# Group norm at the end of an RWKV recurrence: variances spread over channels by one product, root and reciprocal taken on 128x512

## The chip, the cores and the metric

The kernel runs on one core of one Trainium2 chip (trn2). The metric is the device time of one launch in microseconds, the median of several runs.

## The reference, cut to what matters

One layer of a streaming encoder over 1024 tokens of 1024 channels: a hybrid time mixer (RWKV-7 beside stick-breaking attention), a norm, an MLP, a norm. The change touches one thing in the RWKV branch, the norm of each head's answer over its 64 channels, and what follows it:

```python
RWKV_HEADS = 8; HEAD_DIM = 64; GN_EPS = 64e-5

def _group_norm(y, g, b):
    mu = jnp.mean(y, axis=-1, keepdims=True)
    var = jnp.mean(jnp.square(y - mu), axis=-1, keepdims=True)
    return (y - mu) * lax.rsqrt(var + GN_EPS) * g.reshape(RWKV_HEADS, HEAD_DIM) + b.reshape(RWKV_HEADS, HEAD_DIM)

y = _rwkv7_scan(rh, heads(decay), kh, vh, -kk, kk * ah)
y = _group_norm(y, rw_gn_g, rw_gn_b)
y = y + jnp.sum(rh * kh * rw_rk, axis=-1, keepdims=True) * vh
y_a = (y.reshape(bsz, s_len, D_RWKV) * g) @ w_branch_a
```

## The kernel before, in words

The program is six phases one after another: the start (conditioning, first norm, first projections), the recurrence, stick-breaking attention, the merge of both branches, the output projection with its norm, and the MLP. Only the recurrence (`phase_recurrence`) is changed. It lies between about 140 and 528 us of the span.

Data lies with channels on the 128 partitions and tokens along the free dimension. A tile of 128 channels is two heads of 64. The recurrence has 512 channels, so four pairs of heads, and 1024 tokens, so two halves of 512: eight **turns**, 0 to 7, each for one pair of heads and 512 tokens. A turn is long and its work is pipelined over later turns by hand. In the code of turn t, `n` is t+1 (whose decays and keys are prepared), `l` is t-1 (whose chain of states is run, in eight steps `chain(l, c)` and `state(l, c)`), `ll` is t-2 (whose answers are centred, squared and summed to variances) and `lll` is t-3 (whose norm is closed). So turns 3 to 7 close the norms of turns 0 to 4. The last three are closed after turn 7, in a stretch where TensorE computes the values' projection (lines 1961, 192 products) in 24 thirds, with the steps left over between them (`steps`).

Each engine runs its own list in the order that its function `turn(t)` writes; there is no scheduler. A `wait(engine, t, name)` holds the engine, and everything behind it in its list, until the count of the semaphore `name` has come to turn t. Each turn also inverts the triangular blocks of its own tokens by four rounds in which TensorE and VectorE alternate: `correction(t, k)` and `corrected(t, k)` on TensorE (lines 1784 and 1793), `inverse(t, k)` on VectorE (lines 1490 and 1492, signals `Te` and `TTe`). `correction(t, k)` can't start before `inverse(t, k-1)` has signalled `Te`. Between them TensorE does pieces of a dense projection (line 1628) in turns 1 to 6; turn 7 has none.

The closing norm of a turn goes like this before the change:

- ScalarE copies the answers to `ysb`; TensorE `centre` (line 1691) takes each head's mean away; ScalarE writes `yc` (line 1214) and its squares into `ysb` again (line 1220).
- TensorE `variance` (line 1699), at the end of the turn: four products, each with 128 tokens of `ysb` as the stationary side and two columns of 0 and 1 as the moving side. They leave 128x8 sums in the bank `TL`: tokens on the partitions, a column for each head and block of 128 tokens.
- In the next turn, ScalarE `deviation` (line 1226) takes the square root on 128x8 into `ri`, behind `state_maps` and in front of `correction(t, 0)`, and VectorE `inverse_deviation` (line 1458) its reciprocal, in front of `state0`.
- TensorE `deviations`, by `spread` (line 1656): eight products with one column of `ri` broadcast to 64 as the stationary side and the identity as the moving side, which turn the 128x8 numbers into 128x512 in `TL`, a token's number in all 64 channels of its head. It stands behind `correction(t, 1)` and in front of `chain(l, 1)`.
- VectorE `normalised` (line 1465), between `state(l, 1)` and `inverse(t, 1)`, multiplies `yc` by `TL`. Later `gained`, `added` and `gated` (lines 1471, 1478, 1485) finish it, with the gate's product (`gate`, line 1715) from TensorE.

An fp32 product of 128x512 is two instructions in the trace, and so is each of the smaller fp32 products.

## Time and profile before

| | |
|---|---|
| median of 3 runs | 1754.0 us (1753.24 to 1755.06) |
| the profiled execution, its own time | 1754.57 us |
| its span, first to last instruction | 1752.8 us |
| busy: PE, PEld | 1654.6 us (94%), 863.8 us (49%) |
| busy: DVE, ACT, POOL | 764.3 us (44%), 561.3 us (32%), 452.3 us (26%) |
| mean granted clock of TensorE | 0.986 of full speed |

PE is TensorE's products, PEld its loads of the stationary side, DVE is VectorE, ACT ScalarE, POOL GpSimd, SP SyncE. "L1656" is line 1656 of the kernel. A row's `out<-in` names the tiles: `rw_tail` is the bank `TL`, `rw_state` the banks of the chain of states, `rw_invx` and `rw_inv` the banks of the inversion, `rec_ri` is `ri`, `rec_ysb` is `ysb`, `rec_yc` is `yc`, `rec_st` the states, `rec_X` and `rec_T` tiles of the inversion. The granted clock (PEclk) is 1.00 at 2.4 GHz and 0.50 at 1.2 GHz. The bracket at a row's end is how long its engine stood idle before it and what ended that.

### The profile page before, as it was taken

The page shows a single profiled execution, that of the slowest core. Times are in us where ns is not written, and L with a number is a line of the kernel's source. Part 1 is how long each engine was busy: PE and PEld are TensorE (multiplying, and loading weights), DVE is VectorE, ACT ScalarE, POOL GpSimd, SP SyncE. Part 2 cuts the span into 40 slices and gives each one's busy share as a digit, 9 for nine tenths or more (in the row PEclk, how much of TensorE's full clock was granted, in tenths as well). Part 3 has the DMA queues.
Part 4 walks back from the last instruction along what each step waited for, and adds up shares of the span by engine and source line. Part 5 has one row for each costly group of instructions (what it writes and reads, how often), then busy time and mean ns, then how long its engine had stood idle before and what let it go on. Part 6 is the DMA issues. An engine that isn't in the chain of part 4 may idle for free. (4 is left out here: it accounts for less than half of the span.)

```text
span 1752.8 us, 35509 instructions
## 1 busy us (share of the span) xinstructions
PE 1654.6 (94%) x15497; PEld 863.8 (49%) x15690; DVE 764.3 (44%) x1045; ACT 561.3 (32%) x883; POOL 452.3 (26%) x236
## 2 busy tenths in 40 slices
PE   4998889899999998899999999999999999999997
PEld 2455666666644555444444345444444444444443
DVE  5696555556425555312210388331323323222328
ACT  5323444444324555321212256321212112121200
POOL 2221322222110112022422123551423233232310
PEclk9999999999999999999999999999999999999999
DMA  9851001000101200411210211330202020212002
GB/s 358 285 175 32 15 6 38 4 27 27 28 25 49 61 1 1 137 44 36 72 36 24 96 49 37 103 129 21 85 20 76 24 72 26 70 36 84 1 0 97
DMA packets 105777, 109.75 MB, mean 63 GB/s; under 512 B 2592, under 2 KB 82610, under 8 KB 105394
## 3 DMA queue, kind: packets, MB, share of 16 engines
q1 hardware_dynamic: 105648, 107.82, 19.0%
q8 instruction: 107, 1.75, 0.4%
q14 instruction: 22, 0.18, 0.0%
HBM read 101.52 MB, written 4.19 MB: 60 GB/s over the span
## 5 line engine op out<-in xcount | busy, mean ns | idle before, releaser
L218 PE MATMUL tokens_ps<-a_hi,z 128*128 128x512 bf16 x878 | 228.5, 379 | 0.9
L674 PE MATMUL ff_ps<-ff_hi,c_lo 128*128 128x512 bf16 x503 | 190.6, 379 | 0.6
L674 PE MATMUL ff_ps<-ff_hi,c_hi 128*128 128x512 bf16 x501 | 189.9, 379 | 1.3 <-DVE z L2582 0.9
L674 PE MATMUL ff_ps<-ff_lo,c_hi 128*128 128x512 bf16 x501 | 189.9, 379 | 0.6
L2582 DVE TENSOR_TENSOR z<-ff_ps,z 128x512 f32<-128x512 f32 x128 | 88.3, 690 | 205.1 <-PE ff_ps L674 204.4
L2478 ACT ACTIVATE ff_r<-tokens_ps,cols 128x1024 f32<-128x1024 f32 x30 | 33.4, 1113 | 421.4 <-PE tokens_ps L218 414.4
L2404 POOL TENSOR_TENSOR z<-z 128x1024 bf16<-128x1024 f32 x28 | 62.1, 2219 | 345.5 <-ACT z L2400 345.5
L218 PEld LDWEIGHTS tokens_ps<-a_hi,z 128*128 128x128 bf16 x896 | 87.7, 98 | 105.7
L2570 DVE TENSOR_TENSOR ff_r<-ff_r 128x1024 f32<-128x1024 f32 x32 | 41.1, 1284 | 219.4 <-ACT ff_r L2478 219.4
L218 PE MATMUL tokens_ps<-a_lo,z 128*128 128x512 bf16 x438 | 131.1, 379 | 0.5
L195 POOL TENSOR_TENSOR mg_wlo<-mg_stage,mg_whi 128x1024 bf16<-128x1024 f32 x21 | 45.7, 2178 | 158.2 <-ACT mg_whi L191 158.2
L2515 POOL TENSOR_TENSOR c_lo<-ff_r,c_hi 128x1024 bf16<-128x1024 f32 x32 | 75.7, 2366 | 29.4 <-ACT c_hi L2482 29.4
L674 PEld LDWEIGHTS ff_ps<-ff_hi,c_hi 128*128 128x128 bf16 x512 | 50.1, 98 | 61.7 <-issue 1.3
L218 PE MATMUL mg_ps<-a_hi,mg_whi 128*128 128x512 bf16 x253 | 76.0, 381 | 4.4 <-POOLq L88 4.3
L674 PEld LDWEIGHTS ff_ps<-ff_hi,c_lo 128*128 128x128 bf16 x512 | 50.1, 98 | 60.4
L674 PEld LDWEIGHTS ff_ps<-ff_lo,c_hi 128*128 128x128 bf16 x512 | 50.1, 98 | 60.3
L218 PE MATMUL mg_ps<-a_hi,mg_wlo 128*128 128x512 bf16 x250 | 75.7, 383 | 0.3
L218 PE MATMUL mg_ps<-a_lo,mg_whi 128*128 128x512 bf16 x249 | 75.1, 381 | 0.4
L2128 DVE TENSOR_TENSOR mg_ga<-mg_ga,mg_ps 128x1024 f32<-128x1024 f32 x7 | 8.5, 1221 | 143.7 <-PE mg_ps L218 143.7
L805 DVE TENSOR_TENSOR_SCAN b_lo<-z,sb_ahead 128x256 f32<-128x256 f32 (+3 forms) x32 | 53.2, 1704 | 41.2 <-ACT z L909 41.2
L218 PEld LDWEIGHTS tokens_ps<-a_lo,z 128*128 128x128 bf16 x448 | 43.8, 98 | 52.9
L2520 POOL TENSOR_TENSOR ff_lo<-ff_st,ff_hi 128x1024 bf16<-128x1024 f32 x32 | 68.0, 2156 | 0.0
(395 smaller groups left out, 3114.2 us busy)
## 6 DMA issues: line engine op xcount, KB each, us to landing
ff_st<-w_ff SPq DMA_DIRECT2D x8, 2048.0 KB, 7.7
z<-w_ff SPq DMA_DIRECT2D x30, 512.0 KB, 4.0
ada_w<-w_ada SPq DMA_DIRECT2D x6, 2048.0 KB, 8.3
z<-w_in SPq DMA_DIRECT2D x18, 512.0 KB, 4.9
z<-w_ada SPq DMA_DIRECT2D x8, 1024.0 KB, 13.4
mg_stage<-w_in SPq DMA_DIRECT2D x16, 512.0 KB, 3.9
zs_stage<-w_in SPq DMA_DIRECT2D x8, 512.0 KB, 7.3
ada_w<-w_ada SPq DMA_DIRECT2D x4, 1024.0 KB, 13.5
```

Source lines behind the costliest of these rows:

```text
L195: pool.tensor_tensor(lo[u][:], stage[u][:], hi[u][:], ALU.subtract).then_inc(lo_ready[u], 1)
L218: last = pe.matmul(out[:, h * HALF:(h + 1) * HALF], w[:, kt, :], a[:, slot, h * HALF:(h + 1) * HALF], start=(x == 0 and y == 0), stop=(x = ...
L674: last = pe.matmul(out, a[:, slot, at], w[:, x, n], start=(x == 0 and y == 0), stop=(x == k - 1 and y == 2))
L805: dve.tensor_tensor_scan(prod[b][:, 0:nk][:, ::-1], m, masked, 1.0, ALU.mult, ALU.max).then_inc(s_scan, 1)
L2128: dve.tensor_tensor(ga[:], ga[:], ps[2][:], ALU.mult).then_inc(s_pa, 1)
L2404: pool.tensor_tensor(ff.lo[u], stage[u], ff.hi[u], ALU.subtract).then_inc(ff.lo_ready[u], 1)
L2478: act.activation(r[u][:], (wide if begun and t >= begun else ps1)[u][:], ACT.Relu, bias=g.cols[:, ds(gr * GT + (b1 + t), 1)]).then_inc(s_r ...
L2515: pool.tensor_tensor(g.c_lo[:, GT * par + t, :], r[u][:], g.c_hi[:, GT * par + t, :], ALU.subtract).then_inc(s_ulo[u], 1)
L2520: pool.tensor_tensor(lo2[par][:, k, :], st2[:, k, :], hi2[par][:, k, :], ALU.subtract).then_inc(s_o2, 1)
L2570: dve.tensor_tensor(r[u][:], r[u][:], r[u][:], ALU.mult).then_inc(s_sq[u], 1)
L2582: dve.tensor_tensor(acc, ps2[x % 4], acc, ALU.add).then_inc(s_acc, 1)
```

## The change

`variance` is one product of 128x512: the stationary side is `bones`, the 128x128 matrix that has 1 where row and column belong to the same head, and the moving side is `ysb`. Each channel of a head so gets the head's sum of squares, for every token. `deviation` takes the square root on 128x512, from `TL` back into `ysb`. `inverse_deviation`, `deviations` and `spread` go, with `ri` and the semaphore `rb`. `normalised` first takes the reciprocal of `ysb` on 128x512, in place, and then multiplies `yc` by `ysb`. `gate` waits for the root (`sd`) in place of `normalised`'s signal (`y1`), and `answers` waits for `y1` of two turns before in place of `var`, since `ysb` is in use until then. In the stretch after turn 7 the same calls go.

```diff
--- before.py
+++ after.py
@@ -972,7 +972,7 @@
         wc = [sb(f"wc{f}", (P, NC)) for f in range(2)]
         bt, kt_, bh, kh = (sb(n) for n in "bt kt bh kh".split())
         kn, vn = (sb(n, (P, NT, P)) for n in "kn vn".split())
-        rn, ri = [sb(f"rn{f}", (P, NB)) for f in range(2)], sb("ri", (P, NB))
+        rn = [sb(f"rn{f}", (P, NB)) for f in range(2)]
         W, mk = ([c[:, at:at + 2, :].rearrange("p a n -> p (a n)").bitcast(F32).rearrange("p (b x n) -> p b x n", x=2, n=CH)
                   for at in (PAIRS, PAIRS + 2)] for c in (g.c_hi, g.c_lo))
         NTd, NTm = sb("NTd", (P, NB, CH)), sb("NTm", (P, NB, 3, B))
@@ -986,7 +986,7 @@
                     "ch": NC, "S": NC}
         names = ("gs du draw dz dhi dlo vs vz vdif vcopy kkr sq lw sg la a cum cumE eN eE eI t k2 aN ss ssm rn AT RT BT KT wc rk BhT KhT M0 pp TT0 M1e NTd NTm TTe Te "
                  "M2 M2e X Xe TX X21 X21e TTm T12 T12e vnT vne knT kne bnT bne anT ane mv mve PQ PQa PQd ZG ze ge HY S0 ch S out ysb cen yc sqy "
-                 "var sd ri rb y1 y2 bo bv gm y3 y4 yhi ylo vw vhi vlo vmm vout").split()
+                 "var sd ri y1 y2 bo bv gm y3 y4 yhi ylo vw vhi vlo vmm vout").split()
         s = {n: nc.alloc_semaphore(f"rws_{n}") for n in names}
         DENSE = len(DENSE_STAGE)
         s_din = {d: nc.alloc_semaphore(f"rws_din{d}") for d in range(2, DENSE)}
@@ -1202,7 +1202,7 @@
                 if not inside(l):
                     return
                 wait(act, l, "out")
-                wait(act, l - 2, "var")
+                wait(act, l - 2, "y1")
                 for c2 in range(2):
                     act.activation(c8(ysb[l % 2])[:, c2::2, :], half4(HY[c2], 1), ACT.Copy).then_inc(s["ysb"], 1)
 
@@ -1223,7 +1223,7 @@
                 if not inside(l):
                     return
                 wait(act, l, "var")
-                act.activation(ri[:], TL[:, 0:NB], ACT.Sqrt, bias=g.misc(4), scale=1.0 / HD).then_inc(s["sd"], 1)
+                act.activation(ysb[l % 2][:], TL[:], ACT.Sqrt, bias=g.misc(4), scale=1.0 / HD).then_inc(s["sd"], 1)
 
             def high(ll):
                 if not inside(ll):
@@ -1451,18 +1451,14 @@
                 shifted(dve, 8, l)
                 dve.tensor_tensor(rk[l % 4][:], TL[:], zs(8, l), ALU.mult).then_inc(s["bv"], 1)
 
-            def inverse_deviation(l):
-                if not inside(l):
-                    return
-                wait(dve, l, "sd")
-                dve.reciprocal(ri[:], ri[:]).then_inc(s["ri"], 1)
-
             def normalised(ll):
                 if not inside(ll):
                     return
-                wait(dve, ll, "rb")
+                wait(dve, ll, "sd")
                 wait(dve, ll, "yc")
-                dve.tensor_tensor(yc[ll % 2][:], yc[ll % 2][:], TL[:], ALU.mult).then_inc(s["y1"], 1)
+                dve.reciprocal(ysb[ll % 2][:], ysb[ll % 2][:]).then_inc(s["ri"], 1)
+                wait(dve, ll, "ri")
+                dve.tensor_tensor(yc[ll % 2][:], yc[ll % 2][:], ysb[ll % 2][:], ALU.mult).then_inc(s["y1"], 1)
 
             def gained(ll):
                 if not inside(ll):
@@ -1515,7 +1511,6 @@
                 queries(l, 0)
                 for e in range(2):
                     dve.tensor_tensor(W[f][:, 4 * e:4 * e + 4, 0, :], half4(BAB[e], 1), over(incl, NT), ALU.mult).then_inc(s["M1e"], 1)
-                inverse_deviation(lll)
                 state0(l)
                 write_hats(t)
                 inverse(t, 0)
@@ -1570,7 +1565,6 @@
             queries(end, 1)
             queries(end, 0)
             state0(end)
-            inverse_deviation(end - 2)
             normalised(end - 2)
             state(end, 0)
             gained(end - 2)
@@ -1581,7 +1575,6 @@
             bonus(end - 1)
             for c in range(3, 7):
                 state(end, c)
-            inverse_deviation(end - 1)
             state(end, 7)
             normalised(end - 1)
             gained(end - 1)
@@ -1590,7 +1583,6 @@
             bonus(end)
             wait(dve, end, "bv")
             dve.memset(vd[0:1, :, 0:P], 0.0).then_inc(s["vz"], 1)
-            inverse_deviation(end)
             normalised(end)
             gained(end)
             added(end)
@@ -1650,13 +1642,6 @@
                     last = pe.matmul(TL[:, 2 * j:2 * j + 2], tmp[:, j * P:(j + 1) * P], g.const[:, CT["misc"], 0:2], start=True, stop=True)
                 last.then_inc(s["ss"], 1)
 
-            def spread(dst, small, done):
-                for j in range(NT):
-                    for e in range(2):
-                        last = pe.matmul(dst[heads[e], j * P:(j + 1) * P], small[:, 2 * j + e:2 * j + e + 1].to_broadcast([P, HD]), ident,
-                                         start=True, stop=True)
-                last.then_inc(s[done], 1)
-
             def chain(l, c):
                 if not inside(l):
                     return
@@ -1695,23 +1680,15 @@
                     return
                 wait(pe, l, "yc")
                 wait(pe, l, "sqy")
-                for j in range(NT):
-                    last = pe.matmul(TL[:, 2 * j:2 * j + 2], ysb[l % 2][:, j * P:(j + 1) * P], g.const[:, CT["misc"], 0:2], start=True, stop=True)
-                last.then_inc(s["var"], 1)
-
-            def deviations(ll):
+                pe.matmul(TL[:], bones, ysb[l % 2][:], start=True, stop=True).then_inc(s["var"], 1)
+
+            def gate(ll):
                 if not inside(ll):
                     return
-                wait(pe, ll, "ri")
+                pe.wait_ge(s["gs"], 16)
+                wait(pe, ll, "sd")
                 if inside(ll + 4):
                     wait(pe, ll + 4, "sg")
-                spread(TL, ri, "rb")
-
-            def gate(ll):
-                if not inside(ll):
-                    return
-                pe.wait_ge(s["gs"], 16)
-                wait(pe, ll, "y1")
                 pe.matmul(TL[:], g_s[:, ll // 2 * P:(ll // 2 + 1) * P], zgs[:, tok(ll)], start=True, stop=True).then_inc(s["gm"], 1)
 
             def bonus(l):
@@ -1850,7 +1827,6 @@
                     dense(2, 0, 8)
 
                 correction(t, 1)
-                deviations(lll)
                 chain(l, 1)
                 if t:
                     dense(2 * n, 20, 24)
@@ -1934,17 +1910,14 @@
             state_terms(end)
             answer_terms(end)
             steps = {1 + c: [lambda c=c: chain(end, c)] for c in range(NC)}
-            steps[0] = [lambda: deviations(end - 2)]
             steps[1] += [lambda: gate(end - 2)]
             steps[3] += [lambda: bonus(end - 1)]
             steps[4] += [lambda: centre(end - 1)]
             steps[6] += [lambda: variance(end - 1)]
-            steps[8] += [lambda: deviations(end - 1)]
             steps[9] = [lambda: outputs(end), lambda: gate(end - 1)]
             steps[11] = [lambda: bonus(end)]
             steps[12] = [lambda: centre(end)]
             steps[14] = [lambda: variance(end)]
-            steps[16] = [lambda: deviations(end)]
             steps[17] = [lambda: gate(end)]
             pe.wait_ge(s["vlo"], KT)
             for tt in range(TT):
```

On VectorE, turn 5. `rec_st` is the states of the chain, `rec_T` and `rec_TT` the inversion. Before:

```order
L1444 TENSOR_TENSOR rec_zt<-rw_inv,rec_ar 128x4x64
L1517 TENSOR_TENSOR c_hi<-rw_main,const 128x4x64 x2
L1458 RECIPROCAL rec_ri<-rec_ri 128x8
L1427 MEMSET rec_st 128x64
L1412 TENSOR_TENSOR rec_bh<-rec_bt,rec_wc 128x512
L1490 TENSOR_TENSOR rec_T<-rw_invx,rec_T 128x256
L1492 STREAM_TRANSPOSE rec_TT<-rec_T 128x256
L1496 TENSOR_TENSOR c_lo<-rw_main,const 128x512 x2
L1435 SCALAR_TENSOR_TENSOR rec_st<-rec_st,rec_wc,rw_state 128x64
L1417 TENSOR_TENSOR rec_kh<-rec_kt,rec_wc 128x512
L1435 SCALAR_TENSOR_TENSOR rec_st<-rec_st,rec_wc,rw_state 128x64
L1465 TENSOR_TENSOR rec_yc<-rec_yc,rw_tail 128x512
```

And from the last of these states on, after the change:

```order
L1435 SCALAR_TENSOR_TENSOR rec_st<-rec_st,rec_wc,rw_state 128x64
L1459 RECIPROCAL rec_ysb<-rec_ysb 128x512
L1461 TENSOR_TENSOR rec_yc<-rec_yc,rec_ysb 128x512
L1486 TENSOR_TENSOR rec_T<-rw_invx,rec_T 128x256
L1488 STREAM_TRANSPOSE rec_TT<-rec_T 128x256
```

The small reciprocal at the turn's start is gone, and one of 128x512 stands directly in front of the multiplication, with the inversion's next round behind both.

On TensorE, turn 5, from the products of the inversion's `correction(t, 1)` to the gate's. Before:

```order
L1784 MATMUL rw_invx<-rec_T,rec_NTm 32x32 x32
L1656 MATMUL rw_tail<-const,rec_ri 64x128 x8
L1670 MATMUL rw_state<-rec_st,rec_gt 64x64 x2
L1628 MATMUL rw_front<-a_hi,z 128x512 x2
L1628 MATMUL rw_front<-a_lo,z 128x512
L1628 MATMUL rw_front<-a_hi,z 128x512
L1793 MATMUL rw_invx<-rec_X,rec_TT 32x32 x32
L1772 MATMUL rw_main<-const,z 128x128 x4
L1670 MATMUL rw_state<-rec_st,rec_gt 64x64 x2
L1784 MATMUL rw_invx<-rec_T,rec_NTm 32x32 x32
L1715 MATMUL rw_tail<-z,rec_g_s 128x512
```

After:

```order
L1761 MATMUL rw_invx<-rec_T,rec_NTm 32x32 x32
L1655 MATMUL rw_state<-rec_st,rec_gt 64x64 x2
L1620 MATMUL rw_front<-a_hi,z 128x512 x2
L1620 MATMUL rw_front<-a_lo,z 128x512
L1620 MATMUL rw_front<-a_hi,z 128x512
L1770 MATMUL rw_invx<-rec_X,rec_TT 32x32 x32
L1749 MATMUL rw_main<-const,z 128x128 x4
L1655 MATMUL rw_state<-rec_st,rec_gt 64x64 x2
L1761 MATMUL rw_invx<-rec_T,rec_NTm 32x32 x32
L1692 MATMUL rw_tail<-z,rec_g_s 128x512
```

The eight spreading products are gone from between the correction and the chain's step, and nothing else moves.

## Rows read from the trace of the kernel before

**Rows 1.** Busy by stage: window, length, PE, PEld, DVE, ACT, POOL; PEclk, DMA, GB/s.
```profile
350.00:391.00 41.00, 38.22 (x1090) 27.25 (x1098) 23.05 (x49) 19.96 (x37) 9.74 (x7) 0.96 0.10 29
...
392.00:394.00 2.00, 2.00 (x96) 1.81 (x96) 0.00 (x0) 0.00 (x0) 0.00 (x0) 0.50 0.04 8
```

**Rows 2.** Whom TensorE waited for, 265 to 470 us: total, times, longest.
```profile
PE rw_front L1628 <- POOL z L1097: 4.5, 3, 1.5
```

**Rows 3.** Timeline of turn 5: start, duration, engine, line, operation, idle before.
```profile
363.78 1.09 PE L1656 MATMUL rw_tail<-const,rec_ri 128*64 128x128 f32 x16
...
364.81 0.33 PE L1670 MATMUL rw_state<-rec_st,rec_gt 64*64 64x64 f32 x4
...
365.19 0.28 DVE L1435 SCALAR_TENSOR_TENSOR rec_st<-rec_st,rec_wc,rw_state 128x64 f32<-128x64 f32 x1 [1.17 <-PE rw_state L1670]
...
365.38 0.68 DVE L1465 TENSOR_TENSOR rec_yc<-rec_yc,rw_tail 128x512 f32<-128x512 f32 x1
...
366.83 0.42 DVE L1490 TENSOR_TENSOR rec_T<-rw_invx,rec_T 128x256 f32<-128x256 f32 x1 [0.77 <-PE rw_invx L1793]
...
367.31 0.33 PE L1670 MATMUL rw_state<-rec_st,rec_gt 64*64 64x64 f32 x4
...
367.57 0.62 PE L1784 MATMUL rw_invx<-rec_T,rec_NTm 32*32 32x32 f32 x50
```

**Rows 4.** Groups by line and form on VectorE, whole run: busy us, mean ns.
```profile
L2287 DVE RECIPROCAL ou_rs<-ou_rs 128x1 f32<-128x1 f32 x16 | 2.6, 164 | 8.8 <-ACT ou_rs L2245 8.8
...
L1384 DVE RECIPROCAL rec_rn<-rec_rn 128x8 f32<-128x8 f32 x8 | 1.6, 203 | 0.3
...
L2552 DVE RECIPROCAL ff_rs<-ff_rs 128x1 f32<-128x1 f32 x8 | 1.2, 156 | 0.0
...
L568 DVE RECIPROCAL rs<-rs 128x1 f32<-128x1 f32 x8 | 0.9, 115 | 0.1
```

**Rows 5.** Timeline of turn 7, where TensorE waits for VectorE.
```profile
457.96 0.68 DVE L1452 TENSOR_TENSOR rec_rk<-rw_tail,z 128x512 f32<-128x512 f32 x1
...
458.80 1.10 PE L1691 MATMUL rw_tail<-rec_ysb,const 128*128 128x512 f32 x2 [0.19 <-DVE rec_rk L1452]
```

**Rows 6.** Timeline of turn 7, around the spreading.
```profile
445.44 1.98 PE L1656 MATMUL rw_tail<-const,rec_ri 128*64 128x128 f32 x16
...
447.34 0.48 PE L1670 MATMUL rw_state<-rec_st,rec_gt 64*64 64x64 f32 x4
...
447.87 0.28 DVE L1435 SCALAR_TENSOR_TENSOR rec_st<-rec_st,rec_wc,rw_state 128x64 f32<-128x64 f32 x1 [2.58 <-PE rw_state L1670]
...
449.76 0.60 ACT L1190 ACTIVATE rec_vn<-rw_main 128x512 f32<-128x512 f32 x1 [3.80 <-PE rw_main L1772]
...
449.92 0.75 PE L1784 MATMUL rw_invx<-rec_T,rec_NTm 32*32 32x32 f32 x64
```

**Rows 7.** Timeline of turn 7, the root on ScalarE and who waits behind it.
```profile
439.27 0.27 ACT L1226 ACTIVATE rec_ri<-rw_tail,const 128x8 f32<-128x8 f32 x1
...
439.87 0.32 PE L1793 MATMUL rw_invx<-rec_X,rec_TT 32*32 32x32 f32 x15 [0.75 <-ACT rec_X L1186]
```

**Rows 8.** Timeline of the stretch after turn 7.
```profile
469.00 1.09 PE L1656 MATMUL rw_tail<-const,rec_ri 128*64 128x128 f32 x16 [0.46 <-POOL z L1111]
...
472.24 0.28 DVE L1435 SCALAR_TENSOR_TENSOR rec_st<-rec_st,rec_wc,rw_state 128x64 f32<-128x64 f32 x1 [1.41 <-PE rw_state L1670]
...
474.90 0.33 PE L1670 MATMUL rw_state<-rec_st,rec_gt 64*64 64x64 f32 x4
```

**Rows 9.** Timeline of TensorE, the same products in turns 2 and 5.
```profile
189.57 0.69 PE L1808 MATMUL rw_main<-rec_ar,rec_bt 64*64 64x64 f32 x32
...
191.90 0.64 PE L1745 MATMUL rw_state<-rec_PQ,c_hi 64*64 64x64 f32 x32
...
350.52 1.13 PE L1808 MATMUL rw_main<-rec_ar,rec_bt 64*64 64x64 f32 x32
...
354.18 0.63 PE L1745 MATMUL rw_state<-rec_PQ,c_hi 64*64 64x64 f32 x32
```

More of the change, by code:

```diff
@@ L1697, in variance @@
                 wait(pe, l, "sqy")
-                for j in range(NT):
-                    last = pe.matmul(TL[:, 2 * j:2 * j + 2], ysb[l % 2][:, j * P:(j + 1) * P], g.const[:, CT["misc"], 0:2], start=True, stop=True)
-                last.then_inc(s["var"], 1)
-            def deviations(ll):
-                if not inside(ll):
-                    return
-                wait(pe, ll, "ri")
-                if inside(ll + 4):
-                    wait(pe, ll + 4, "sg")
-                spread(TL, ri, "rb")
+                pe.matmul(TL[:], bones, ysb[l % 2][:], start=True, stop=True).then_inc(s["var"], 1)
             def gate(ll):
@@ L1713, in gate @@
                 pe.wait_ge(s["gs"], 16)
-                wait(pe, ll, "y1")
+                wait(pe, ll, "sd")
+                if inside(ll + 4):
+                    wait(pe, ll + 4, "sg")
                 pe.matmul(TL[:], g_s[:, ll // 2 * P:(ll // 2 + 1) * P], zgs[:, tok(ll)], start=True, stop=True).then_inc(s["gm"], 1)
```

## The prediction

> **What bounds the kernel now.** I read the busy time by stage first. In turn 5, which stands for turns 3 to 6, TensorE is busy 38.2 of 41 us and VectorE 23.1 [rows 1]: TensorE sets the pace, VectorE has room on average. The waits of TensorE come second. Between 265 and 470 us the largest sum is 4.5 us in three waits for GpSimd at the start of a turn; for VectorE it waits once, 0.2 us [rows 5]. So before the change VectorE is never late. The third view is the timeline around the spreading, since a mean over a turn doesn't tell whether VectorE may be late at this one place. There the engines hand work to each other at short distances [rows 3]: the spreading starts at 363.78, the chain's step at 364.81, VectorE's state step at 365.19 (it had waited for it), its multiplication at 365.38, and TensorE needs the inversion's next round for its correction at 367.57. From the state step to that correction it is 2.38 us. What VectorE does in between must fit there.
>
> **What TensorE saves.** The spreading takes 364.81 - 363.78 = 1.03 us in a turn at full clock [rows 3], and 447.34 - 445.44 = 1.90 us in turn 7, where it ran at the lower clock [rows 6]. There are eight: turns 3 to 6, turn 7, and three after it. The variance product replaces four products with 128 columns of stationary side each by one of 128x512. An fp32 product of 128x512 is in these traces about as long as the spreading (1.10 us with its modelled end [rows 5]; the spreading 1.09 [rows 3]); the old variance is of the same kind, eight small instructions. I take no difference, 0.3 us either way in all. At the ends of turns 3 to 6 it is hidden anyway, for TensorE waits there for another engine, GpSimd in three of the four [rows 2].
>
> **The root on ScalarE.** It takes 0.27 us on 128x8 [rows 7]; a pass over 128x512 out of PSUM takes 0.60 [rows 6], so +0.33. In turns 3 to 6 TensorE's next product that waits for ScalarE comes later than that. In turn 7 it doesn't: TensorE waited for the copy right behind the root [rows 7]. There 0.33 us lie on the path. After turn 7 nothing of TensorE's is behind it.
>
> **The reciprocal on VectorE.** This is the unknown. The trace has no reciprocal of 128x512, but has small ones [rows 4]: 203 ns for 128x8, 164 and 156 for 128x1 in two places, 115 in a third. From one element to eight it grows by 39 to 47 ns, so 5.6 to 6.7 ns for each element. For 512 elements that makes 203 ns + 504 x 5.6 to 6.7 ns = 3.0 to 3.6 us; I take 3.3, the middle. The third place would give (203 - 115)/7 = 12.6 ns and 6.5 us, the upper bound. The lower is an operation that takes an element in the same time as the multiplication next to it: 0.68 us [rows 3]. I stay with the two rows that are nearest to each other, since slopes over seven elements are weak evidence and these two agree.
>
> The page "VectorE: DVE Perf Modes" of the Trainium skill, in "Walkthrough: the 8-slice pipeline in each mode", speaks against this change: the reciprocal is iterated, with a repeat count of 8, where an addition needs one stage. As an estimate from that page's 0.96 GHz it would be 8.3 ns an element, some 4.5 us, and the sum below would come to +9.4 in place of +3.4. The trace agrees that an element costs several times an ordinary one, but its slope is below 8.3 ns.
>
> **What it delays, in turns 3 to 6.** Behind the state step, VectorE now does: 0.19 us until the next operation starts (365.38 - 365.19 [rows 3]), 3.3 reciprocal, 0.68 multiplication (it reads SBUF in place of PSUM; GpSimd is idle then), 0.42 for the addition that signals `Te` (at 366.83 [rows 3]), and 0.16 from VectorE's end to TensorE's start (457.96 + 0.68 to 458.80 [rows 5]). That is 4.75 us in place of the 2.38: TensorE stands 2.37 us longer there. But it had reached the chain's step 1.03 us sooner. Net +1.34 a turn, 4 x 1.34 = **+5.4**. What is queued behind on VectorE (state steps, the cumulative sum, later rounds) moves by the same amount within 0.2 us, and so do ScalarE and GpSimd, which feed on it. So I see nothing that gives it back at the turn's end: GpSimd's late weights there follow ScalarE, and ScalarE follows TensorE.
>
> **Turn 7.** From the state step at 447.87 to the correction at 449.92 it is 2.05 us [rows 6]: 4.75 - 2.05 - 1.90 = +0.80, with the root's 0.33 **+1.1**.
>
> **After turn 7.** TensorE has dense products, and the spreads go: 3 x 1.03 = **-3.1**. What hides the reciprocal: the first one stands in front of the state step that released the chain's next step at 474.90. The multiplication would start about 471.5 (root's end about 468.1, plus 3.3), and the state step be done by 472.4, while TensorE comes to that next step at 474.90 - 1.03 = 473.87 [rows 8]: 1.4 us to spare. The second and third reciprocal stand behind the last state steps, and their results are needed 4 us or more later. So the cover holds up to a reciprocal of about 4.7 us; beyond, each further microsecond costs one.
>
> **Sum.** +5.4 + 1.1 - 3.1 = +3.4 us, and 5 us for each microsecond of the reciprocal: +1.9 at 3.0 us, +4.9 at 3.6. It breaks even at 2.6 us. Then the clock. In turn 6 TensorE ran at half clock for some microseconds (0.50, that is 1.2 GHz [rows 1]), after a wait of 1.5 us [rows 2] and before small products. The same products take 191.90 - 189.57 = 2.33 us at full clock and 354.18 - 350.52 = 3.66 in turn 5 after such a wait [rows 9]: 1.3 us for a fall. The new wait in turns 3 to 6 is from 367.31 + 0.33 - 1.03 = 366.61 to 367.57 + 1.34 = 368.91 [rows 3], 2.3 us, longer than those. I expect one or two falls in five turns, +2.0, between none and four (+5.2). Total +5.4. The sum stands against the profiled execution, 1754.57 us: 1760.0. The median of the runs is 0.57 lower, 1754.0, so the forecast is **1759.4 us**.
>
> **Rivals.** *One: the reciprocal is an ordinary pass.* If the slope of rows 4 is only start-up and 128x512 takes 0.68 us, the list behind the state step is 2.13 us, shorter than 2.38, and all savings count: 4 x -1.03, in turn 7 -1.90 + 0.33, after it -3.1, together -8.8: **1745.2 us**, faster. It decides below 2.6 us of reciprocal. For it: 115 to 203 ns are mostly fixed time, and VectorE's wide operations all lie at 0.7. Against: two slopes that agree at about six times the usual. Chance 0.13. The same page, in "The TRN2 errata", has a fixed cost and one element a cycle for VectorE's SBUF operations, which by its formula is 0.59 us for 512.
>
> *Two: it is slower still*, 4.5 us or up to 6.5. Then 3.4 + 5 x 1.2 = +9.4, with the falls +11.4, **1765.4 us**; at 6.5 us +16.0 more than at 3.3, 1.9 after turn 7, with falls 1777. For it: the third row of rows 4; against: its other two. Chance 0.12.
>
> *Three: the new wait is partly a gift.* TensorE's waits at the starts of turns (4.5 us [rows 2]) and its short stops for nothing visible could shrink by what it stands elsewhere, where their causes run ahead; that would take 2 to 5 us off: **1755.5 us**, level, perhaps below before. Against: those causes hang on TensorE themselves, as far as I followed them. Chance 0.13.
>
> The forecast's own case has 0.62, and runs from 1755.9 (3.0 us, no fall) to 1764.1 (3.6 us, four falls).
>
> **How the numbers follow.** A measurement of this kernel tells 0.2%, 3.5 us, from no change. Of the forecast's case 0.40 lies above that and 0.22 within. Rival one is faster (0.13), rival two slower (0.12), rival three 0.04 faster, 0.06 within, 0.03 slower. Together 0.17, 0.28, 0.55. The range 1751 to 1767 takes in the whole first case, most of rival three and rival two up to some 4.7 us, and leaves out rival one and the top of two, 0.19.
>
> **What would show it.** In the profile after: eight reciprocals of 128x512 at 3.0 to 3.6 us; no rows of 128*64 products into `rw_tail`; in turns 3 to 6 a wait of TensorE's correction for VectorE's addition of 2.0 to 2.7 us; distance from turn to turn 1.3 us longer, more where PEclk shows a fall; the stretch after turn 7 shorter by 3 us; every later phase unchanged. Wrong it would be with a reciprocal below 2.6 us, or with that wait there and the turns no longer.

## The result and the profile after

The changed kernel takes 1772.8 us (median of 4 runs, 1769.61 to 1776.29), the kernel before 1754.3 us on the same chip: a ratio of 1.0106, 95% interval 1.0086 to 1.0126. That is slower, as forecast, but by 18.4 us where 5.4 were forecast, and above the range. The profiled execution took 1772.95 us. Its page, the head and the instruction queue of the DMA section:

```profile
span 1771.2 us, 35345 instructions
...
PE 1675.3 (95%) x15514; PEld 853.9 (48%) x15514; DVE 784.3 (44%) x1045; ACT 565.8 (32%) x883; POOL 452.6 (26%) x236
...
q8 instruction: 123, 2.02, 0.5%
```

VectorE works 20 us more. TensorE's busy time reads 20.7 us higher, though its work became less. That can't be read as a rise, for the two traces don't hold the same share of the products. A product and its weight load come in pairs, and here both count 15514, while before the change 193 of the products have no record:

```profile
PE 1654.6 (94%) x15497; PEld 863.8 (49%) x15690; DVE 764.3 (44%) x1045; ACT 561.3 (32%) x883; POOL 452.3 (26%) x236
```

The one profile of the kernel before (with idle instructions, below) that has all its records shows 1678.0 us.

The last line of the page above counts packets and MB of the queue that brings the instructions; the same line of the kernel before is this:

```profile
q8 instruction: 107, 1.75, 0.4%
```

The program became shorter by 357 TensorE instructions, and fetched 16 packets more. The prediction does not use this line.

The groups of VectorE and ScalarE between 265 and 535 us (line, operation, form, times | busy us, mean ns):

```profile
L1459 DVE RECIPROCAL rec_ysb<-rec_ysb 128x512 f32<-128x512 f32 x8 | 26.8, 3347 | 8.8 <-ACT rec_ysb L1226 8.8
...
L1461 DVE TENSOR_TENSOR rec_yc<-rec_yc,rec_ysb 128x512 f32<-128x512 f32 x8 | 5.5, 691 | 0.3
L1226 ACT ACT_TABLE_LOAD x5 | 6.4, 1283 | 0.1
L1226 ACT ACTIVATE rec_ysb<-rw_tail,const 128x512 f32<-128x512 f32 x8 | 5.5, 686 | 0.8 <-PE rw_tail L1683 0.7
```

The reciprocal takes 3.35 us (forecast 3.3), the root 0.69 (0.60). Whom TensorE waited for between 265 and 490 us (total, times, longest), which answers to [rows 2]:

```profile
PE rw_invx L1761 <- DVE rec_T L1486: 11.4, 5, 3.3
PE rw_front L1620 <- POOL z L1097: 3.6, 3, 1.2
```

The first line is the new wait of the forecast, in all five turns. The timeline of turn 5 shows it, and what follows ([rows 3] are its counterparts):

```profile
368.74 3.35 DVE L1459 RECIPROCAL rec_ysb<-rec_ysb 128x512 f32<-128x512 f32 x1
372.12 0.69 DVE L1461 TENSOR_TENSOR rec_yc<-rec_yc,rec_ysb 128x512 f32<-128x512 f32 x1
372.73 0.42 DVE L1486 TENSOR_TENSOR rec_T<-rw_invx,rec_T 128x256 f32<-128x256 f32 x1
...
373.20 0.99 PE L1761 MATMUL rw_invx<-rec_T,rec_NTm 32*32 32x32 f32 x64 [2.01 <-DVE rec_T L1486]
374.13 2.08 PE L1692 MATMUL rw_tail<-z,rec_g_s 128*128 128x512 f32 x2
```

TensorE stands for 2.01 us, and the gate's product behind it takes 2.08 us. By the windows before and from there on (length, PE busy, PEclk, DMA, GB/s) the clock had fallen to 1.2 GHz for most of 4 us:

```profile
365.00:373.00 8.00, 6.18 (x209) 1.00 0.02 4
373.00:377.00 4.00, 3.80 (x72) 0.57 0.00 0
```

Where the 18.4 us lie is read from landmarks, operations that both kernels have: the 128x8 reciprocal of each turn, the closing memset, the first LayerNorm reciprocal after the output projection, and the first one after the MLP. Before the change (times, ns, first and last start):

```profile
L1384 DVE RECIPROCAL rec_rn<-rec_rn x8: 203/203/203, 154.8 to 419.2; 128x8 f32<-128x8 f32 x8
L793 DVE MEMSET sb_ahead<- x1: 805/805/805, 528.3 to 528.3; 128x896 f32 x1
L2287 DVE RECIPROCAL ou_rs<-ou_rs x16: 162/164/165, 998.4 to 1085.7; 128x1 f32<-128x1 f32 x16
L2552 DVE RECIPROCAL ff_rs<-ff_rs x8: 155/156/158, 1710.1 to 1748.0; 128x1 f32<-128x1 f32 x8
```

After it:

```profile
L1384 DVE RECIPROCAL rec_rn<-rec_rn x8: 203/203/204, 154.7 to 430.6; 128x8 f32<-128x8 f32 x8
L793 DVE MEMSET sb_ahead<- x1: 805/805/805, 539.1 to 539.1; 128x896 f32 x1
L2260 DVE RECIPROCAL ou_rs<-ou_rs x16: 163/164/166, 1007.7 to 1095.0; 128x1 f32<-128x1 f32 x16
L2525 DVE RECIPROCAL ff_rs<-ff_rs x8: 154/156/158, 1728.4 to 1766.4; 128x1 f32<-128x1 f32 x8
```

At the end of the recurrence the change is 10.8 us behind, 9.3 after the output projection, and 18.3 after the MLP. (The part between the first two took 468.6 to 471.3 us in the 18 profiles, so the 1.5 us there are spread.) So there are **two losses of about the same size**: one in the recurrence, and one of 9.1 us in the MLP, of whose code the diff touches nothing. There TensorE has two waits that the kernel before has not, 170 us apart, each directly behind the first two products of the loop's body:

```profile
1298.82 1.01 PE L218 MATMUL tokens_ps<-a_lo,z 128*128 128x512 bf16 x2 [2.38 <-issue]
1469.25 1.01 PE L218 MATMUL tokens_ps<-a_lo,z 128*128 128x512 bf16 x2 [2.64 <-issue]
```

and low clock behind each:

```profile
1299.00:1304.00 5.00, 5.00 (x18) 0.72 0.01 3
...
1469.00:1474.00 5.00, 4.75 (x15) 0.66 0.01 3
```

### The profile page after: what moved, and what is told of

It reads as the page before. It is cut to its first block and busy times, and to the rows that moved or that the text cites. A ratio compares the mean times of both kernels' runs of the same rounds, so it can differ in the third digit from the quotient of the medians.

```text
span 1771.2 us, 35345 instructions
## 1 busy us (share of the span) xinstructions
PE 1675.3 (95%) x15514; PEld 853.9 (48%) x15514; DVE 784.3 (44%) x1045; ACT 565.8 (32%) x883; POOL 452.6 (26%) x236
## 3 DMA queue, kind: packets, MB, share of 16 engines
q8 instruction: 123, 2.02, 0.5%
## 5 line engine op out<-in xcount | busy, mean ns | idle before, releaser
L218 PE MATMUL tokens_ps<-a_hi,z 128*128 128x512 bf16 x896 | 232.8, 381 | 0.4 <-issue 0.4
L674 PE MATMUL ff_ps<-ff_hi,c_hi 128*128 128x512 bf16 x512 | 194.0, 379 | 0.9 <-DVE z L2555 0.9
L674 PE MATMUL ff_ps<-ff_lo,c_hi 128*128 128x512 bf16 x512 | 194.0, 379 | 0.0
L218 PE MATMUL tokens_ps<-a_lo,z 128*128 128x512 bf16 x448 | 134.7, 383 | 5.0 <-issue 5.0
L1620 PE MATMUL rw_front<-a_hi,z 128*128 128x512 bf16 x224 | 76.5, 396 | 3.9 <-POOL z L1097 3.6
```

What stands on the lines that cost most here:

```text
L218: last = pe.matmul(out[:, h * HALF:(h + 1) * HALF], w[:, kt, :], a[:, slot, h * HALF:(h + 1) * HALF], start=(x == 0 and y == 0), stop=(x = ...
L674: last = pe.matmul(out, a[:, slot, at], w[:, x, n], start=(x == 0 and y == 0), stop=(x == k - 1 and y == 2))
L1620: mm = pe.matmul(unit_bank(u)[:], w_part[:, kt, :], a_part[:, kt, h * HALF:(h + 1) * HALF], start=(x == 0), stop=(x == 3 * KT - 1))
```

## The theories

**Theory A, the place of the code.** The change takes 88 fp32 products and, by a count of the program, five wait instructions out of TensorE's stream. The rows count two passes a product (x16 for eight in [rows 3]), each with its weight load, so four instructions: 88 x 4 + 5 = 357. Everything behind moves forward by these. The MLP's loop is 1581 instructions by the same count and runs three times, so it jumps back twice: the two waits. 2.02 MB in 123 packets are 16.4 KB each, which is 256 instructions if one has 64 bytes, and 1581 is 6 x 256 + 45: the loop touches 7 such pieces, or, if it starts in one of the last 44 places of a piece, 8. Two jumps that fetch 8 pieces each would be the 16 packets more. **Theory B**: the loop loses it by something else that the change does.

The Trainium skill, "Runtime: NRT & Kernel Launch", section "Instruction fetch mechanics", gives TensorE 128 KiB for instructions, refilled in blocks of 256, and says that a taken branch forces a fetch when its target isn't in the current window of two pages; it counts the crossing of a block as mostly hidden. The block size agrees with the packets. By the window of two pages every jump of this loop would stall, which the runs below don't bear out. By the 128 KiB, which would be 8 blocks, a loop that touches 8 would fit; that is not borne out either, if the start that stalls is one that touches 8. How much a jump costs the page doesn't say, the runs below do.

For the recurrence, **theory one** is the forecast's: VectorE is late at one place of the turn because of the 3.35 us. **Theory two**: the loss comes from the root, from the missing products, or from the code's place.

The kernel before was timed again on the chip of each of these runs, at medians of 1754.8 to 1755.2 us; the ratios are to these.

## First four: code restored, reciprocal out, reciprocal early

Idle TensorE instructions ("fillers") in `phase_start`, where TensorE waits anyway, put the later code back. A 32x32 product is four instructions. Of two `wait_ge` one is left as an instruction of its own, of six three, and a single one adds none:

```diff
+            for fill in range(89):
+                quarter = slice(32 * (fill % 4), 32 * (fill % 4) + 32)
+                pe.matmul(ada_ps[1][quarter, 0:32], g.const[quarter, CT["ident"], quarter], g.const[quarter, CT["ident"], quarter], start=True, stop=True)
+            for fill in range(2):
+                pe.wait_ge(s_const, 16)
```

> The change, with 357 TensorE instructions that compute nothing needed put into phase_start, where TensorE is idle for about 14 us: every later TensorE instruction stands again where it stood before the change, which had removed 357. Two theories share the 18.4 us that the change cost. Of both, the recurrence keeps its +10.8 (end of the phase 539 against 528 us). Theory A, the MLP loop lost its 9 us by where its instructions lie: from the first MLP reciprocal (1007.7 after, 998.4 before) the lead stays the same to the end, the waits of the loop's first product on issue (5.4 us each at most) are gone, and the time is 1763.5 (1762 to 1765). Theory B, the loop lost it by something else that the change does (a clock that stays lower, DMA queues): the waits stay, 1772.8 as the change itself.

Measured: 1764.8 us (1761.1 to 1766.0), ratio 1.0051 [1.0034, 1.0067]. The MLP's stretch, from first to first landmark, is 711.7 us, as before the change (720.8 in the change), and the queue has 107 packets. The loss is gone with every instruction of the change still there, so **B falls**; the next run makes it without the change.

> The kernel before, with 155 idle TensorE instructions in phase_start: modulo 256 instructions (16 KB, what one packet of the instruction queue carries) every later instruction then lies as it does in the change, which has 357 fewer. Theory A with a rule of 16 KB pieces: the MLP loop shows the issue waits and the time is 1763 (+9). Theory A without such a rule (the absolute place, or the order of fetches, decides): anything from +0 to +9. Theory B, placement does nothing: 1754.3, within 1 us of before.

38 products and six waits in the kernel before: 1763.5 us, ratio 1.0049 [1.0033, 1.0066]; nothing that computes had changed. Its recurrence ends 2.3 us earlier than in the kernel before, its MLP stretch is 719.7 us. It waits at both jumps, 2.44 and 1.97 us; the first, and the queue:

```profile
1287.82 1.01 PE L218 MATMUL tokens_ps<-a_lo,z 128*128 128x512 bf16 x2 [2.44 <-issue]
```

```profile
q8 instruction: 125, 2.05, 0.5%
```

The MLP's loss is so made without the change, and taken from it: **theory A holds.** The next kernel leaves the reciprocal out and multiplies by the deviation itself, so it computes something else:

```diff
-                dve.reciprocal(ysb[ll % 2][:], ysb[ll % 2][:]).then_inc(s["ri"], 1)
-                wait(dve, ll, "ri")
```

> As the filled change, but the 128x512 reciprocal is left out: the closing norm multiplies by the deviation instead of its inverse, every TensorE instruction is the same. Theory one, the reciprocal is what TensorE waits for in turns 3 to 7: each of these turns gets 3.3 us of VectorE back, no wait of the correction product on inverse(t, 0) beyond 1 us, no half clock behind it; recurrence ends some 6 us before that of before (turns -1.03 each and the end -3.1), 1747 (1744 to 1750). Theory two, the loss comes from elsewhere (the missing spreading products leave gaps, the wide root on ScalarE): less than half of the recurrence's +10.8 comes back, 1758 or more.

Measured: 1752.4 us, ratio 0.9987 [0.9978, 0.9997]. The time is above the 1744 to 1750, but the stretch it speaks of is right: from the landmark of turn 0 to the end of the phase 367.4 us, against 373.6 in the kernel before (-6.1) and 381.6 with the reciprocal. Eight reciprocals cost 14.2 us there. TensorE's wait for VectorE is gone, and of the five stretches of low clock between 265 and 500 us one is left, of 11 us where it had 15. **Theory one holds**: the root and the missing products are in this kernel too. What the expectation missed lies outside the recurrence: its landmark of turn 0 comes 2.0 us later than in the kernel before, and the part from the memset to the output projection took 1.1 us more. Both lie within the spread of single executions: that landmark comes at 153.9 to 158.9 us in the 18 profiles, and at 156.8 and 154.9 in two of one kernel.

In the last of the four, the root comes before `state_maps` on ScalarE and the reciprocal at the very start of VectorE's turn:

```diff
-                state_maps(l)
                 deviation(lll)
+                state_maps(l)
...
+            def inverse_deviation(l):
+                if not inside(l):
+                    return
+                wait(dve, l, "sd")
+                dve.reciprocal(ysb[l % 2][:], ysb[l % 2][:]).then_inc(s["ri"], 1)
...
             def turn(t):
...
+                inverse_deviation(lll)
                 wait(dve, t, "M0")
```

> As the filled change, but the root of a finished turn stands first on ScalarE and its 128x512 reciprocal first on VectorE, where VectorE waits about 6 us for M0 at the start of the next turn; the same work is done. Theory one (it is the place of the 3.345 us, not their amount, that costs): TensorE's wait on inverse(t, 0) falls to at most 0.5 us, the recurrence ends about 2 to 6 us before that of before, 1748 (1745 to 1753). Theory two (VectorE has no slack in a turn, the 3.3 us must be paid anywhere): as the filled change, 1762 to 1764.

Measured: 1754.1 us, ratio 0.9994 [0.9983, 1.0005]. That is 1 us above the expected range. Of the 12.3 us between the filled change and the one without a reciprocal the place alone gives back 10.6, with all eight reciprocals done. The order shows a price of its own (TensorE's waits, 265 to 490 us):

```profile
PE rw_invx L1775 <- ACT rec_gt L1205: 4.0, 2, 2.6
```

ScalarE's copy, which TensorE waits for here, had itself waited for VectorE. The longer of the two, in turn 7:

```profile
435.17 3.35 DVE L1464 RECIPROCAL rec_ysb<-rec_ysb 128x512 f32<-128x512 f32 x1 [4.21 <-ACT rec_ysb L1232]
438.44 0.69 DVE L1512 TENSOR_TENSOR rec_NTd<-rw_main,rec_rn 128x256 f32<-128x256 f32 x2
...
440.75 0.41 DVE L1450 TENSOR_TENSOR rec_zt<-rw_invx,rec_ar 128x256 f32<-128x256 f32 x1
...
441.20 0.38 ACT L1205 ACTIVATE rec_gt<-rw_invx 128x256 f32<-128x256 f32 x1 [4.85 <-DVE rec_zt L1450]
```

In turns 3 and 7 the early reciprocal reaches into the start of the inversion on VectorE, and TensorE pays 1.4 and 2.6 us for it.

## Four more: pieces or place, width, one-instruction root

> The change with 101 filler instructions instead of 357: TensorE's instructions after the filler lie at another absolute place than before the change (256 fewer), but at the same place within their 256-instruction, 16 KB pieces. Theory A with pieces (the MLP loop of 1581 instructions touches 7 pieces or 8, and only 7 stay loaded across a jump back): no issue wait at the two jumps back, some 106 packets on the instruction queue, 711.7 us from the first MLP reciprocal to the first closing LayerNorm reciprocal as before the change, time 1763 (1761 to 1765), perhaps 1 us less than with 357 fillers, which cost 2.2 us where they stand. Theory A by absolute place: the waits come back, 720 us for that stretch, 1771 or more.

25 products and two waits. Measured: 1761.2 us (1759.1 to 1766.8), ratio 1.0032 [1.0018, 1.0047]; MLP stretch 711.7 us, 106 packets. It is the place within the piece, and not the absolute place. Fewer fillers did not bring the landmark of turn 0 forward (158.3 us, 157.0 with 357), so the 2.2 us that I had put down to them are not theirs.

> Root and reciprocal early in the turn, with 101 fillers instead of 357. With pieces: the MLP stretch stays 711.7 us and the smaller filler gives back 1 to 1.6 us: 1752.8 (1751 to 1754.5), just below the kernel before. By absolute place: 1761.

Measured: 1752.7 us, ratio 0.9981 [0.9968, 0.9994], MLP stretch 711.7 us. As the piece rule had it.

```diff
-                dve.reciprocal(ysb[ll % 2][:], ysb[ll % 2][:]).then_inc(s["ri"], 1)
+                dve.reciprocal(ysb[ll % 2][:, 0:HALF // 2], ysb[ll % 2][:, 0:HALF // 2]).then_inc(s["ri"], 1)
```

`HALF` is 512.

> The filled change with only half of each reciprocal done (columns 0 to 255; the other half is multiplied by the deviation itself), everything else the same. Between 1764.8 with the whole and 1752.4 with none. Theory one, TensorE waits for VectorE at the same point of every turn as soon as VectorE has more work: the time follows the width, 1.67 of 3.34 us, so half of the 12.4 us comes back, 1758.6 (1757.5 to 1760). Rival, VectorE has a slack of 1 to 1.7 us in a turn and the clock falls only behind a long wait: nearly all comes back, 1754 or less.

Measured: 1753.4 us, ratio 0.9996 [0.9986, 1.0006]. The expected 1758.6 was wrong, and the rival holds: half the reciprocal costs nearly nothing. Turns 3 to 6 together take 163.2 us, the same as with none. VectorE has a slack there, and only what goes beyond it is paid. The waits that are left (265 to 490 us):

```profile
PE rw_invx L1767 <- DVE rec_T L1492: 2.4, 4, 0.6
```

The last of the four changes one function name and drops the reciprocal:

```diff
-                act.activation(ysb[l % 2][:], TL[:], ACT.Sqrt, bias=g.misc(4), scale=1.0 / HD).then_inc(s["sd"], 1)
+                act.activation(ysb[l % 2][:], TL[:], ACT.Abs_reciprocal_sqrt, bias=g.misc(4), scale=1.0 / HD).then_inc(s["sd"], 1)
...
-                dve.reciprocal(ysb[ll % 2][:], ysb[ll % 2][:]).then_inc(s["ri"], 1)
-                wait(dve, ll, "ri")
```

> The change with 101 fillers, where ScalarE takes the inverse root in one instruction (reciprocal square root of the same 128x512) instead of the root, and VectorE's reciprocal goes. TensorE's and ScalarE's instructions keep their number and place. Theory one: as without the reciprocal, recurrence 6 us shorter than before the change, 1751 (1749.5 to 1753) with the smaller filler. Rival: the new function takes longer than 0.69 us or needs a table load (1.28 us each) more often than the root, which had 5: 1753 to 1760. Its accuracy is open.

Measured: 1750.1 us, ratio 0.9971 [0.9962, 0.9981]. The function costs what the root did, with as many table loads (here in the version with 52 fillers):

```profile
L1232 ACT ACTIVATE rec_ysb<-rw_tail,const x8: 681/687/687, 271.3 to 500.1; 128x512 f32<-128x512 f32 x8
L1232 ACT ACT_TABLE_LOAD  x5: 1283/1283/1283, 270.0 to 430.2; - x5
```

## The edge of the piece, and three quarters of the width

> The one-instruction inverse root without any filler. Piece rule (8 pieces touched by the MLP loop instead of 7): every gain of the recurrence stays, but 16 packets more, two issue waits of about 2.5 us at the jumps back and 720.5 us instead of 711.7 in the MLP stretch: 1758.5 (1757 to 1760), slower than before the change although the recurrence is 6 us shorter. If the filler had helped for another reason: 1750 or less, since its own cost goes.

Measured: 1758.6 us, ratio 1.0016 [1.0006, 1.0025]; MLP stretch 718.4 us, 123 packets, waits at both jumps:

```profile
PE tokens_ps L218 <- issue: 4.5, 2, 2.3
```

> The same with 52 fillers. The runs so far (loop at instruction 112 of a piece: free; at 11: stalls, body of 1581 = 6 pieces and 45) leave 45 starts in 256 that touch an 8th piece; 44 fillers or more are then enough whatever the unknown offset. Piece rule: no stall, 711.7 us in the MLP stretch, 1749.7 (1748 to 1751.5). If it needs the old place: 1758 to 1759.

Measured: **1743.4 us** (1742.6 to 1744.3), ratio 0.9931 [0.9915, 0.9948]; MLP stretch 711.7 us, 105 packets. No stall, as expected; the recurrence is faster still than expected, of which more below.

> The kernel before with 200 idle TensorE instructions; 155 of them had brought the MLP stall (+8 us). 45 more carry the loop's start past the edge of the piece. Piece rule: the stall is gone again, MLP stretch 711.7 us, time 1756 (1754.5 to 1757.5, the filler's own 1 us). Rival, any shift away from a lucky place stalls, or a later place stalls more: 1763.

Measured: 1755.1 us, ratio 1.0001 [0.9992, 1.0011]; MLP stretch 711.7 us, 107 packets. 155 fillers stall, 200 don't. By the rule of pieces that must be so, for the 45 instructions between them are one more than the 44 places that touch an eighth piece. Where exactly these places begin and end no run shows: one start was tried that stalls and five that don't (45, 52, 76, 101 and 153 instructions further on, taken within a piece). Of the 18 profiles those three whose loop starts in the same place of a piece (the change, one_step_root_0, before_shifted) have an MLP stretch of 718.4 to 720.8 us, all the others 711.7.

> Filled change, 384 of the reciprocal's 512 columns (2.51 of 3.34 us), the rest multiplied by the deviation itself. With the half TensorE waited 0.6 us a turn for inverse(t, 0), with the whole 2.2; here 1.4 us. Theory with clock falls (a wait above some length is followed by 4 us at half clock, worth 1.6 us; five such in the whole, one in the half): four or five falls, 1761 (1759.5 to 1762.5). Theory without: only the waits grow, 4 to 5 turns by 0.84 us: 1757.3 (1756 to 1758.5).

Columns 0 to 383. Measured: 1757.9 us (1751.5 to 1760.4), ratio 1.0012 [1.0000, 1.0025]. TensorE waits 1.41 us in each of turns 3 to 6, as expected, but the clock falls behind one of these waits only, and the time lies in the range without falls. Two of the waits, and with the whole reciprocal the first of them:

```profile
286.82 0.85 PE L1767 MATMUL rw_invx<-rec_T,rec_NTm 32*32 32x32 f32 x64 [1.41 <-DVE rec_T L1492]
370.09 0.95 PE L1767 MATMUL rw_invx<-rec_T,rec_NTm 32*32 32x32 f32 x64 [1.41 <-DVE rec_T L1492]
```

```profile
285.82 1.08 PE L1767 MATMUL rw_invx<-rec_T,rec_NTm 32*32 32x32 f32 x64 [2.20 <-DVE rec_T L1492]
```

The windows around these waits, turns 3 to 6, with three quarters:

```profile
284.00:290.00 6.00, 4.59 (x147) 1.00 0.02 5
328.00:334.00 6.00, 5.30 (x150) 1.00 0.01 3
371.00:375.00 4.00, 4.00 (x16) 0.57 0.02 4
414.00:420.00 6.00, 6.00 (x154) 1.00 0.01 3
```

and with the whole:

```profile
285.00:289.00 4.00, 3.18 (x70) 0.57 0.01 4
330.00:334.00 4.00, 3.83 (x69) 0.60 0.00 0
374.00:378.00 4.00, 3.67 (x16) 0.57 0.01 4
419.00:422.00 3.00, 2.67 (x9) 0.51 0.00 0
```

Behind 2.2 us of waiting the clock fell in all four turns, behind 1.4 in one of four. Turns 3 to 6 take 174.3 us with the whole and 167.2 with three quarters. Of the 7.1 us between them 3.2 are waits (4 x 0.8, from 1.41 to 2.21); the other 3.9 go with three more falls, **1.3 us each**, the figure that the forecast had taken from [rows 9].

## What was left of the recurrence

> The change itself with 52 fillers. MLP stretch 711.7 us by the piece rule. If the start of the recurrence's code is worth 6 to 7 us: 1755 (1753.5 to 1757); if that gain belongs to the one-instruction root alone or to that chip: 1761 as with 101 fillers.

Measured: 1761.9 us, ratio 1.0037 [1.0025, 1.0049], as with 101 fillers. MLP stretch 711.7 us.

> The kernel before with the same 52 fillers. If the start of the recurrence is what counts and not its length: 1748 to 1750; if the place of every piece edge inside the turns counts (they lie otherwise here, 357 instructions more in the turns): anything between 1750 and 1757, most likely 1754.8.

Measured: 1752.9 us, ratio 0.9987 [0.9971, 1.0003]. Within the noise of no effect.

> The one-instruction root with 76 fillers, halfway between 52 (1743.4) and 101 (1750.1). If placement moves the recurrence's time steadily: 1746.5 (1745 to 1748.5); if it goes by steps: 1743.5 or 1750.

Measured: 1747.6 us, ratio 0.9952 [0.9938, 0.9966].

> The same kernel as one_step_root_52, on the chip of the three others of this call: 1743.4 (1742.5 to 1745) if the gain is the code's, 1749 to 1750 if it was the chip's.

Measured: 1745.6 us, ratio 0.9945 [0.9929, 0.9962]. Neither bound of the expectation: 2 us above the first time, still 4.5 below 101 fillers. The ratios go from 0.9931 and 0.9945 over 0.9952 to 0.9971 with 52, 76 and 101 fillers, so the start of the code seems to matter to this kernel by some 4.5 to 7 us (76 fillers lie in the range of a steady move); the change and the kernel before show no such gain with 52. TensorE's waits for nothing visible, in front of the correction (235 to 535 us), first with 52 and then with 101 fillers:

```profile
PE rw_invx L1765 <- issue: 2.0, 2, 1.3
```

```profile
PE rw_invx L1765 <- issue: 5.6, 6, 1.4
```

fit with that, but which instruction stalls on which fetch the runs did not show.

The stretches in one table (us; filler instructions ahead of the recurrence; the phase from the landmark of turn 0 to its end). They are those of one profiled execution each, which can lie some us from the median of its kernel (with the change and 101 fillers it took 1766.8 us, with the one-step root and none 1754.6):

| kernel | fillers | turns 3 to 6 | phase | MLP stretch | median |
|---|---|---|---|---|---|
| before | 0 | 166.4 | 373.6 | 711.7 | 1754.3 |
| the change | 0 | 178.6 | 384.5 | 720.8 | 1772.8 |
| the change | 52 | 173.8 | 379.5 | 711.7 | 1761.9 |
| the change | 101 | 176.4 | 382.4 | 711.7 | 1761.2 |
| the change | 357 | 174.3 | 381.6 | 711.7 | 1764.8 |
| 3/4 reciprocal | 357 | 167.2 | 375.3 | 711.7 | 1757.9 |
| 1/2 reciprocal | 357 | 163.2 | 369.2 | 711.7 | 1753.4 |
| no reciprocal | 357 | 163.2 | 367.4 | 711.7 | 1752.4 |
| early | 357 | 165.6 | 371.3 | 711.7 | 1754.1 |
| one-step root | 0 | 162.2 | 367.9 | 718.4 | 1758.6 |
| one-step root | 52 | 159.8 | 361.5 | 711.7 | 1743.4 |
| one-step root, again | 52 | 160.7 | 364.5 | 711.7 | 1745.6 |
| one-step root | 76 | 159.3 | 366.5 | 711.7 | 1747.6 |
| one-step root | 101 | 163.4 | 368.3 | 711.7 | 1750.1 |

In the change, fillers shorten the phase by 2 to 5 us too. So of the recurrence's 10.8 us some 8 are the reciprocal's net effect (6 to 9 in the three filled versions), and the rest, 2 to 5, goes with the place of the code or with the spread of single profiles; these two I can't tell apart.

## Why the prediction was wrong, step by step

- **The reciprocal**: 3.3 us taken, 3.35 measured, from two slopes over seven elements. Over the 504 further elements the slope is 6.2 ns. By the repeat count of the Trainium skill, "VectorE: DVE Perf Modes", section "Walkthrough: the 8-slice pipeline in each mode", it would have been 8.3. Rivals one and two had rested on other durations, and are out. Right.
- **The new wait**: 2.0 to 2.7 us forecast; 1.69, 2.21, 2.01 and 2.21 in turns 3 to 6 (and 3.25 in turn 7). Right in three of four turns.
- **Turns 3 to 6**: +5.4 and, with the falls, up to +7.4 was the sum. With the later code in its old place they are 7.9 longer (7.3 and 10.0 in the other two filled versions); in the change itself 12.2. The mechanism is right, and for the filled change the sizes too: four falls of the clock in these turns against two before the change, at 1.3 us each, turn the +5.4 into +8.0. In the change itself the clock falls five times there, which makes +9.3; 2.9 us stay open. The break-even at 2.6 us, which was that of the whole sum, came a little too high: with 2.51 us of reciprocal the sum gives about half a microsecond below the kernel before, and the ratio is 1.0012 [1.0000, 1.0025], so 0 to 4 us above.
- **The clock**: 1.3 us a fall was right. The new wait brought a fall in every turn, where I had taken one or two in five; but falls of the kernel before, at the starts of turns, went. From 265 to 500 us the traces show low clock in four stretches before (20 us together), six in the change (29) and five in the filled change (32, of which 15 are one stretch in turn 7). With some 4 us a fall that is two to three falls more, so 2.6 to 3.9 us where +2.0 was taken: somewhat under-sized.
- **The root and turn 7**: the root takes 0.69 us where 0.60 was taken, so +0.42 for +0.33. From the landmark of turn 7 to the correction behind the new wait it is 30.7 us before and 31.5 in the change, +0.8, where +1.1 was forecast. Right. Behind the wait the clock falls once more:

```profile
462.11 1.08 PE L1761 MATMUL rw_invx<-rec_T,rec_NTm 32*32 32x32 f32 x64 [3.25 <-DVE rec_T L1486]
463.11 2.08 PE L1692 MATMUL rw_tail<-z,rec_g_s 128*128 128x512 f32 x2
```

  The rest of the turn takes 1.7 us longer than before, most of it the price of this fall, so turn 7 is +2.5 in all (+3 to +5 in the three filled versions, with 14 to 15 us of low clock near its end against 8). Its end is here the start of the first of the three last spreads, 469.00 us before the change [rows 8], and after it the first value product, at 482.89.
- **After turn 7**: -3.1 forecast; from that first spread to the end of the phase it is 59.3 us before, and from the first value product 56.2 after, -3.1. Right. The cover for the first reciprocal held: TensorE waits there for no state step.
- **"Every later phase unchanged"**: this step failed. It costed the removal of 357 instructions at nothing beyond the time they take, and that removal was worth 9.1 us, half of the result, by where it put the MLP's loop. The view that would have warned was at hand: a loop of 1581 instructions, packets of 256, and a change that moves the loop's start by 357, to a place that with a chance of about one in six (44 of 256) brings an eighth piece. A rival with that chance and +9 us belonged in the text. With it out of the way the filled versions take 1761.2, 1761.9 and 1764.8 us, inside the range and 2 to 5 us above the forecast.
- **Rival three** (the new wait is partly a gift): TensorE's waits for GpSimd at the starts of turns read 4.5 us before and 3.6 in the change, but most of that is the records. Where the first product behind such a wait has no record, the wait reads 0.2 us longer; the trace of the kernel before shows it as 31 stops of the same product for nothing:

```profile
PE rw_front L1628 <- issue: 4.9, 31, 0.2
```

Like with like it is 4.5 against the 4.3 of the filled change, or 3.9 (before_shifted_200) against 3.6. Nothing of the size it needed.

The idea of the change is good where the reciprocal isn't: with the inverse root in one ScalarE instruction and 52 fillers the kernel takes 1743.4 us (1745.6 the second time), by the ratios 0.7 and 0.55% below the kernel before and so 1.6 to 1.7% below the change.

## What to carry to other kernels

A reciprocal on VectorE costs by the elements of a partition, 6.5 ns each at 128x512, so spreading first and inverting afterwards trades eight small products for 3.1 us on VectorE; whether that is paid depends on one place in the turn, not on VectorE's 44% mean. An edit that changes the number of instructions ahead of a long loop (1581 here, 7 pieces or 8) can cost microseconds at every jump back: compare the packets of the instruction queue before and after, and the waits on "issue" at the loop's first instructions. A few idle instructions then tell the two effects apart, and mend the second.

## What I had not expected of the hardware

A loop of 1581 TensorE instructions ran without a stall at its jumps from the five other starts within a piece that were tried, and from one place was fetched anew at both jumps: 16 packets more (18 in before_shifted), 2.0 to 2.6 us of standing at the jump, and with the low clock behind it 3.3 to 4.5 us each (6.7 to 9.1 us for two). And ScalarE's reciprocal square root of 128x512 takes 687 ns, as the root alone, where root and VectorE's reciprocal take 4.03 us in sequence.
